# A two-block forward pass on one core: time-step products turned round, group transposes moved into the next group, gated opening loads, a tail split by token half, and six products of a tile of ones ahead of the first unit

## What is computed

```python
h = rms_norm(x, norm_w)
proj = h @ w_in
sc_b, sc_c, sc_v, sc_z, ssd_z, ssd_xbc, ssd_dt, mq, mz = _split(proj, EVEN_SPLITS)
y_a = sc_b * causal_depthwise_conv(sc_c * sc_v, sc_conv_w) * silu(sc_z)
xbc = silu(causal_depthwise_conv(ssd_xbc, ssd_conv_w) + ssd_conv_b)
dt = softplus(ssd_dt + ssd_dt_bias)                  # 32 time steps for each token
y_b = ssd_chunked(xs, dt, a, bm, cm) + xs * ssd_d    # 4 groups of 8 heads, 2 chunks of 128 tokens
y_b = group_rms_norm(y_b * silu(ssd_z)) * ssd_norm_w
y_m = memory_attention(mq, mem_n, w_mk, w_mv) * silu(mz)
return x + concatenate([y_a, y_b, y_m]) @ w_out
```

## Time and profile before

| | us |
|---|---|
| median of 3 runs (lowest, highest) | 2774.18 (2772.35, 2777.26) |
| the profiled execution's own time | 2776.7 |
| its span | 2775.2 |
| TensorE busy | 2712.0 |
| VectorE busy | 1529.3 |
| ScalarE busy | 1348.5 |

### The profile page before, as it was taken

How to read it: one execution, slowest core, us unless ns; L and a number is a source line. 1 busy time by engine, 2 the same in 40 slices (tenths; PEclk the granted TensorE clock), 3 DMA queues, 4 the chain that set the end, 5 groups by cost and what they waited for, 6 DMA issues and landing times. The chain is left out here.

```text
span 2775.2 us, 36799 instructions
## 1 busy us (share of the span) xinstructions
PE 2712.0 (98%) x12515; PEld 2256.4 (81%) x12515; DVE 1529.3 (55%) x1865; ACT 1348.5 (49%) x1775; POOL 199.4 (7%) x285
## 2 busy tenths in 40 slices
PE   8999999999999999999999999999998999999997
PEld 6788888888888888888888878888777889788886
DVE  5444455656555555554444644436776755556754
ACT  6444455654444444444444544434554445555543
POOL 2100011100000000000000001001100000121100
PEclk9999999999999999999999999999999999999998
DMA  8766666676655565556666766647656666675564
GB/s 310 268 217 217 214 228 210 197 235 216 224 197 189 182 196 187 188 192 207 218 197 216 237 207 206 218 160 242 202 193 203 233 214 213 224 268 191 175 214 157
DMA packets 161355, 586.94 MB, mean 211 GB/s; under 512 B 18928, under 2 KB 18976, under 8 KB 160496
## 3 DMA queue, kind: packets, MB, share of 16 engines
q1 hardware_dynamic: 133488, 485.55, 53.3%
q0 software_dynamic: 27776, 100.15, 10.9%
HBM read 543.63 MB, written 43.56 MB: 212 GB/s over the span
## 5 line engine op out<-in xcount | busy, mean ns | idle before, releaser
L1617 DVE TENSOR_TENSOR w_lo<-raw,w_hi 128x1024 fp32r<-128x1024 f32 x922 | 1124.0, 1224 | 979.9 <-ACT w_hi L1158 973.1
L1158 ACT ACTIVATE w_hi<-raw 128x1024 fp32r<-128x1024 f32 x922 | 968.5, 1059 | 929.6 <-PE acc L703 884.7
L701 PE MATMUL acc<-w_hi,x_t_hi 128*128 128x512 f32 (+1 forms) x2400 | 955.7, 398 | 1.0 <-DVE w_lo L1617 0.9
L703 PE MATMUL acc<-w_hi,x_t_lo 128*128 128x512 f32 (+1 forms) x2400 | 935.8, 390 | 0.0
L702 PE MATMUL acc<-w_lo,x_t_hi 128*128 128x512 f32 (+1 forms) x2400 | 934.6, 389 | 0.0
L703 PEld LDWEIGHTS acc<-w_hi,x_t_lo 128*128 128x128 f32 x2400 | 451.9, 188 | 93.8
L701 PEld LDWEIGHTS acc<-w_hi,x_t_hi 128*128 128x128 f32 x2400 | 452.7, 189 | 92.6 <-DVE w_lo L1617 3.2
L702 PEld LDWEIGHTS acc<-w_lo,x_t_hi 128*128 128x128 f32 x2400 | 452.9, 189 | 90.4 <-issue 1.9
L701 PE MATMUL acc<-w_hi,ff_t_hi 128*128 128x512 f32 x352 | 137.3, 390 | 0.0
L703 PE MATMUL acc<-w_hi,ff_t_lo 128*128 128x512 f32 x352 | 137.0, 389 | 0.0
L702 PE MATMUL acc<-w_lo,ff_t_hi 128*128 128x512 f32 x352 | 136.9, 389 | 0.0
(11 more groups left out here) (371 smaller groups left out, 2627.8 us busy)
## 6 DMA issues: line engine op xcount, KB each, us to landing
raw<-stream SPq DMA_DIRECT2D x922, 512.0 KB, 4.2
d_in<-tile POOLq DMA_DIRECT2D x20, 512.0 KB, 3.6
d_ev<-tile POOLq DMA_DIRECT2D x20, 512.0 KB, 3.7
d_x<-tile POOLq DMA_DIRECT2D x16, 512.0 KB, 4.0
...
```

The lines of the kernel that those rows point to most:

```text
L701: nc.tensor.matmul(out, a_hi, w_hi[:, s, w], start=first and c == 0, stop=False)
L703: mm = nc.tensor.matmul(out, a_lo, w_hi[:, s, w], start=False, stop=last and c == UCH - 1)
L1158: nc.scalar.activation(w_hi[:, u.slot, :], raw[:, u.slot, :], ACT.Copy).then_inc(hi_ready, 1)
L1617: nc.vector.tensor_tensor(w_lo[:, s, :], raw[:, s, :], w_hi[:, s, :].bitcast(F32), ALU.subtract).then_inc(lo_ready, 1)
```

## The change

- Opening: the loads of the memory's rows wait until 3 and 4 units are used. `norm(0)` stands ahead of the `x_c` loads in GpSimd's queue, and `x_c[n]` waits until 12 + n units are used, besides the one before it. ScalarE's and VectorE's work on them (`square`, `mem_out(0)`, `x_high`, `x_low`) moves to later units. ScalarE copies one element of `ones` first of all. TensorE makes six products of the tile `ones` (128 x 128 by 128 x 256, float32) ahead of the first unit; their result is not used.
- `dt`: the weights become the stationary operand (128 columns, of which 32 count) and 256 tokens are streamed, 48 products; VectorE copies the 32 x 256 result and TensorE transposes it twice at p = 1. The later steps move one or two units back, so `d_ac` is stored after p = 7 in place of p = 5.
- Groups: the loops over four groups are written out. The finished group is transposed at p = 2 and p = 4 of the next group (or of `eout`), four transposes each, into `ps_y`.
- The first load of `sc_in` is issued when group 3's products are made (`s_y` = 4), ahead of the last stores of `sc`.
- Tail: the last four units are done first for tokens 0 to 127, then for 128 to 255 (`last_units`), and each half is finished by itself. The weighting by `fin` is done beforehand for blocks 0 to 2; the scaling is shared by VectorE (blocks 0 and 1) and ScalarE (2 and 3); eight stores of 256 KB go out from SyncE's queue. The three units of zeros are gone.

```diff
-N_UNITS = _u + LEAD
+N_UNITS = _u
+SPLIT_T = 4
+AHEAD = 6
...
+        out_v = halves(io["out"])
+        for t in range(TH):
+            for b in (0, 2, 1, 3):
+                s_ = fin_ready if b < 2 else fin_act
+                sp.wait_ge(s_, 2 * t + b % 2 + 1)
+                sp.dma_start(out_v[:, t, b * NBW:(b + 1) * NBW], res[:, b, t, :]).then_inc(fin_out, 16)
+        sp.wait_ge(fin_out, 16 * 8)
...
         pool.dma_start(tile[1][0:8, 0, 0:N_REL], io["rel_bias"]).then_inc(tile_moved[1], 16)
-        pool.wait_ge(raw_landed[0], 16)
         for b in range(2):
-            load_tile(mem_v, At(b), b % 2, [])
+            load_tile(mem_v, At(b), b % 2, [(unit_used, RING + 3 + b)])
         pool.dma_start(col2[:, :], io["conv_cols"]).then_inc(small_in, 16)
         pool.dma_start(rowb[:, :], io["rowb"].partition_broadcast(P)).then_inc(small_in, 16)
...
+        norm(0)
         for n in range(4):
+            pool.wait_ge(unit_used, RING + 12 + n)
             if n:
                 pool.wait_ge(x_in, 16 * n)
             if n == 3:
                 pool.wait_ge(turn_lo, 2 * TURN["mem"] + 2 + 2)
             pool.dma_start(x_c[n][:, :, :], io["x_cols"][:, 4 * n:4 * n + 4, :]).then_inc(x_in, 16)
-        norm(0)
         for b in range(2):
             load_tile(x_v, At(b), b, [(squared, b + 3)])
         pool.dma_start(pl_row[:, :, :], halves(io["p"])).then_inc(late_in, 16)
...
+        def load_short(j):
+            for t in range(TH):
+                pool.dma_start(sc_in[:, t, :, :].rearrange("p a n -> p (a n)"),
+                               ev_v[:, t, 6144 + 2048 * j:6144 + 2048 * (j + 1)]).then_inc(c_in, 16)
+
...
+            if last:
+                pool.wait_ge(s_y, 4)
+                all_stored(STORED["sc"] + 2)
+                load_short(0)
...
-        for j in range(2):
-            if j:
-                pool.wait_ge(c_ut, 2 * j)
-                pool.wait_ge(c_wt, 2 * j)
-            else:
-                pool.wait_ge(turn_lo, 2 * TURN["x4"] + 2)
-            for t in range(TH):
-                pool.dma_start(sc_in[:, t, :, :].rearrange("p a n -> p (a n)"),
-                               ev_v[:, t, 6144 + 2048 * j:6144 + 2048 * (j + 1)]).then_inc(c_in, 16)
+        pool.wait_ge(c_ut, 2)
+        pool.wait_ge(c_wt, 2)
+        load_short(1)
...
-        norm(7)
-        out_v = halves(io["out"])
-        for b in range(4):
-            pool.wait_ge(fin_ready, b + 1)
-            pool.dma_start(out_v[:, :, b * NBW:(b + 1) * NBW], res[:, b, :, :]).then_inc(fin_out, 16)
-        pool.wait_ge(fin_out, 64)
+        for t in range(TH):
+            pool.wait_ge(mean_ready, 8 + t)
+            pool.tensor_tensor(rstd[:, 14 + t:15 + t], mean[:, 14 + t:15 + t], expo[:, 0:1], ALU.pow)\
+                .then_inc(rstd_ready, 1)
...
+        def last_units(u, src, chunk, bank):
+
+            for n in range(SPLIT_T):
+                pe.wait_ge(lo_ready, u + n + 1 + RING)
+            for t in range(TH):
+                out = acc[2 * bank + t][:, :]
+                for n in range(SPLIT_T):
+                    for c in range(UCH):
+                        w = slice(c * NBW, (c + 1) * NBW)
+                        s = (u + n) % RING
+                        k = (chunk + UCH * n) % 20 + c
+                        a_hi = src[0][:, k, t * P:(t + 1) * P]
+                        a_lo = src[1][:, k, t * P:(t + 1) * P]
+                        nc.tensor.matmul(out, a_hi, w_hi[:, s, w], start=False, stop=False)
+                        nc.tensor.matmul(out, a_hi, w_lo[:, s, w], start=False, stop=False)
+                        mm = nc.tensor.matmul(out, a_lo, w_hi[:, s, w], start=False,
+                                              stop=n == SPLIT_T - 1 and c == UCH - 1)
+                mm.then_inc(unit_used, SPLIT_T // TH)
...
+        pe.wait_ge(ones_ready, 1)
+        for _ in range(AHEAD):
+            nc.tensor.matmul(ps_s[:, 0:TOK], ones[:, 0:P], ones[:, :], start=True, stop=True)
...
-        for t in range(TH):
-            for c in range(16):
-                w = slice(32 * c, 32 * c + 32)
-                a_hi, a_lo = (x3_t[x][:, c, t * P:(t + 1) * P] for x in range(2))
-                out = ps_y[:, 32 * t:32 * t + 32]
-                nc.tensor.matmul(out, a_hi, w_hi[:, u.slot, w], start=c == 0, stop=False)
-                nc.tensor.matmul(out, a_hi, w_lo[:, u.slot, w], start=False, stop=False)
-                mm = nc.tensor.matmul(out, a_lo, w_hi[:, u.slot, w], start=False, stop=c == 15)
+        for c in range(16):
+            w = slice(32 * c, 32 * c + P)
+            x_hi, x_lo = (x3_t[x][:, c, :] for x in range(2))
+            out = ps_y[:, 0:TOK]
+            nc.tensor.matmul(out, w_hi[:, u.slot, w], x_hi, start=c == 0, stop=False)
+            nc.tensor.matmul(out, w_lo[:, u.slot, w], x_hi, start=False, stop=False)
+            mm = nc.tensor.matmul(out, w_hi[:, u.slot, w], x_lo, start=False, stop=c == 15)
         mm.then_inc(unit_used, 1)
 
         def time_steps(p):
-            if p == 3:
-
-                pe.wait_ge(dt_v, 3)
+            if p == 1:
+                pe.wait_ge(dt_v, 1)
+                for t in range(TH):
+                    mm = nc.tensor.transpose(ps_y[:, TOK + 32 * t:TOK + 32 * t + 32], dt_t[:, t * P:(t + 1) * P],
+                                             ident[0:32, 0:32])
+                mm.then_inc(pe_once, 1)
+            if p == 5:
...
-            if p == 5:
-                pe.wait_ge(dt_v, 4)
+            if p == 7:
+                pe.wait_ge(dt_v, 5)
                 nc.tensor.transpose(ps_s[0:64, 0:P], acum[:, :], ident[:, :]).then_inc(pe_once, 1)
...
-                pe.wait_ge(dt_v, 6)
-                pe.wait_ge(turn_lo, At(TURN["sy"], i, 1).times(2, 2))
+                pe.wait_ge(dt_v, 7)
+                pe.wait_ge(s_yb, n.times(1, 1))
...
+                pe.wait_ge(turn_lo, 2 * (TURN["sy"] + g) + 2)
                 nc.tensor.matmul(ps_y[:, :], cv[:, 5, P:TOK], st[:, :], start=True, stop=True).then_inc(s_y, 1)
-            if p == 15:
-                turn_tile(At(TURN["sy"], i, 1), yb, s_tile, n.times(1, 1))
-
-        with pe.Fori(0, 4) as i:
-            pair_of("sc", 0, i, 1, 8, x3_t, 0, lambda p: ssd(p, i))
+
+        def turn_group(p, n):
+
+            for h in range(2):
+                if p == 2 + 2 * h:
+                    pe.wait_ge(s_tile, n + 1)
+                    pe.wait_ge(turn_lo, 2 * (TURN["sy"] + n) + h + 2)
+                    for c in range(2):
+                        for t in range(TH):
+                            at = (2 * h + c) * P
+                            mm = nc.tensor.transpose(ps_y[:, (c * TH + t) * P:(c * TH + t + 1) * P],
+                                                     yb[:, t, at:at + P], ident[:, :])
+                    mm.then_inc(turned, 1)
+
+        def sc_beside(p, g):
+            ssd(p, g)
+            if g:
+                turn_group(p, g - 1)
+
+        for g in range(4):
+            pair_of("sc", 2 * g, 0, 0, 8, x3_t, 0, lambda p: sc_beside(p, g))
...
+            turn_group(q, 3)
...
-            for k in range(10):
...
+        last_units(U0["oout"] + 40 - SPLIT_T, o_t, 16 + UCH * (10 - SPLIT_T), (B0["oout"] + 3) % 2)
...
-            if (b, k) in ((0, 3), (0, 4), (1, 0), (1, 1)):
-                n = ((0, 3), (0, 4), (1, 0), (1, 1)).index((b, k))
+            if (b, k) in ((0, 6), (0, 7), (1, 2), (1, 3)):
+                n = ((0, 6), (0, 7), (1, 2), (1, 3)).index((b, k))
                 act.wait_ge(xin_landed[n % 2], 16 * (n // 2 + 1))
                 square(xin[n % 2], 0, At(n), n or None)
-            if (b, k) == (1, 4):
+            if (b, k) == (1, 6):
                 mem_out(0)
-            if b in (1, 2) and k % 2 == 1:
-                x_high(4 * (b - 1) + k // 2)
-            if (b, k) in ((2, 2), (2, 4), (3, 2), (3, 4)):
-                n = ((2, 2), (2, 4), (3, 2), (3, 4)).index((b, k))
+            if b == 2:
+                x_high(k)
+            if (b, k) in ((2, 6), (2, 7), (3, 3), (3, 4)):
+                n = ((2, 6), (2, 7), (3, 3), (3, 4)).index((b, k))
                 act.wait_ge(xin_landed[n % 2], 16 * (LOADED["x"] + n // 2 + 1))
                 square(xin[n % 2], 8, At(n), 4 + n)
 
+        act.wait_ge(ones_ready, 1)
+        nc.scalar.activation(junk[:, 0:1], ones[:, 0:1], ACT.Copy).then_inc(act_once, 1)
...
-        def sc_pair(i, last_group):
+        def high_group(p, n):
+
+            for h in range(2):
+                if p == 2 + 2 * h:
+                    act.wait_ge(turned, 2 * (TURN["sy"] + n) + h + 1)
+                    for c in range(2):
+                        ch = 4 * n + 2 * h + c
+                        last = nc.scalar.activation(z_t[0][:, ch, :], ps_y[:, c * TOK:(c + 1) * TOK], ACT.Copy,
+                                                    scale=gain[:, 96 + ch:97 + ch])
+                    last.then_inc(turn_hi, 1)
...
             if p == 0:
                 summed(At(U0["dt"]))
```

(65 more changed lines are left out.)

153 lines of the change are left out of this document (89 added, 64 removed).

## The result

The changed kernel takes 2758.86 us (median of 5, 2757.64 to 2759.76) beside 2774.18 for the kernel before on the same chip: a ratio of 0.9947, 95% interval 0.9934 to 0.9959. It is faster, by 15.3 us (0.5%) where 31.1 were forecast, and the time lies above the range of 2733 to 2753. Its profiled execution has a span of 2757.1 at a granted clock of 0.993, where before had 2775.2 at 0.989.

What follows compares the result with a forecast made beforehand. TensorE was taken as the bound, 919 units making 2500 us. Terms 11.3 (dt) + 11.7 (groups) + 9.7 (short convolution) + 2.0 (tail) - 3.6 (opening) = 31.1 off 2774.2 gave 2743.1 us, range 2733 to 2753.

Steps and rivals of the forecast that it cites:

- Groups: Turns between groups: moving the transposes to p = 2 and 4 removes TensorE's waits, winning 11.7 us (6 to 13.8).
- Rival B: VectorE becomes the bound in three groups (2.5 each) and at the short convolution (wait of 4): 2751.7 us, chance 0.12.
- Opening: Start until the 28th unit: GpSimd's chain releases TensorE at 93.9 in place of 90.3, losing 3.6 us.
- the silent stream: Opening: SyncE's loads fall silent near 80 us, so the bias loads run almost alone and win 4.6 us.
- rival A: Opening: the chain in GpSimd's queue stays as long as now, losing the whole 10.8: 2750.3 us, chance 0.2.
- Six products: Ahead of the first unit: cost 0, make it 2.9 us sooner, not counted; without them, up to 2.9 later.
- dt: The dt products: 48 of 256 columns take 5.45 us in place of 96 taking 15.48, saving 11.3 (6.1 to 11.5).
- rival D: Weight loads don't overlap with products in dt, which then takes 10.7: 2748.3 us, chance 0.04.
- Short convolution: Start of the short convolution: the earlier `sc_in` load leaves a wait of 1.4 us, winning 9.7 (7 to 11).
- Tail: Kernel's end: finishing by halves saves 5.1 us, less a stand of 2.5 and 0.6 slow clock: wins 2.0 (0 to 5).
- 5.4 to the end of the span: Tail: the time from the last store's landing to the end of the span, in the kernel before.
- the two rows of memory rows: Stretches where memory rows are loaded, at `ein` and at `uq`: forecast 0 each.

Runs made afterwards that it cites:

- experiment 3: The changed kernel with the second half of each group's transposes, copies and low parts at unit 6 of the next group in place of 4: 2748.61 us, ratio 0.9906.
- experiment 6: The changed kernel with the two halves of a group's transposes at units 4 and 6 of the next group: 2761.28 us, ratio 0.9952.
- experiment 11: The changed kernel with the halves of a group's transposes at units 4 and 8 (last group's at 2 and 6): 2749.16 us, ratio 0.9911.
- experiment 4: The changed kernel without the six products of ones ahead of the first unit: 2763.21 us, ratio 0.9962.
- experiment 7: The changed kernel with its eight last stores and the wait for them in GpSimd's queue in place of SyncE's: 2763.14 us, ratio 0.9965.
- experiment 12: The kernel before with its four last stores and the wait for them in SyncE's queue in place of GpSimd's: 2768.78 us, ratio 0.9980.

## Why the prediction was wrong, point by point

- **Groups: the step that failed.** "They now stand at p = 2 and p = 4, when `yb` has long been scaled" asked only whether the source is ready. It did not ask when the target is free. The turn went from two banks to the one bank `ps_y`, so the second half waits for VectorE's low part of the first, which stands behind three rounds of taps and splits. The price was put at 0.5 a group; it was 3.4 of waiting and about 1.6 of slow transposes and products after it. With two units between the halves the wait is there, with four it is gone (experiments 3, 6 and 11). The direct test, a second bank for the second half, was not run. Rival B had VectorE as the bound, but as a late split worth 2.5, not as a bank; the bank was in no rival.
- **Opening: the path was right, a term of it was not.** The chain in GpSimd's queue did set the 28th unit, and the silent stream did win 4.7 at the bias loads where 4.6 was said. That agreement is in part luck: the 4.6 was worked out for 2 MB, and the two loads move 1.5. What failed is "the `x_c` loads, no longer beside a burst of other loads, and the power taken out of the queue I put at 2.6 together". In place of winning 2.6 this part of the chain lost 1.0: 0.8 won by the power, 1.1 at `d_skew`, and 2.8 lost at `d_e`, because the early power also took away the pause of the stream that had covered `d_e` before. The `x_c` loads, 6.7, 6.8 and 5.3 apart where 5.9 was said, and a start 0.9 later put `x_c[3]` 2.0 behind the forecast. So the release was 5.4 late, and the slow products after the longer stand cost 1.0 more than before. The number is nearly rival A's (-10.8 said, -10.1 measured), its mechanism is not: the chain was 3.7 shorter than before, and started later.
- **Six products: counted as nothing by themselves.** In the profile of the changed kernel they made the first unit fast, as said, but the other traces show that they do so only sometimes (experiment 4). The forecast's own "up to 2.9 later" without them is not contradicted; a fast first unit was worth some 2 us at the 28th.
- **dt was right** (11.3 said, 11.1 in the profile). 48 products took 5.70 where 5.45 was taken, 0.119 each, with their 48 weight loads busy for 5.67 of it, so the loads overlapped and rival D (10.7) falls. The Trainium skill's "TensorE: Matmul & The Clock Gate", section "The mechanism", has them overlap only where the row groups differ; here every product takes all rows, and the trace does not agree with that sentence. The same section allows the overlap for the background weight buffer too; which of the two it is here, the trace doesn't show.
- **Short convolution was right** (9.7 said, 9.0 in the profile). Its wait was 1.1 where 1.4 was said, and the later `sc_in` chain on VectorE was what came next.
- **Tail: right in its parts, one part unseen.** The stand of 2.5 was there (2.56), with eight slow products among those after it, 1.7 in place of 0.6. Saved on the way from TensorE's end to the last issue: 4.9, where 5.1 was said. But "5.4 to the end of the span", taken as fixed, went as well, because the last wait left GpSimd's queue: 4.6 us. Experiments 7 and 12 show it from both sides, 4.3 and 4.5 by the medians. Why the program ends later behind a wait in GpSimd's queue, no run shows.
- In the sum by the profiles: groups 12.5 short, opening 6.5 short, dt and short convolution 0.9 short, tail 3.5 over, and the two rows of memory rows 3.5 over: 12.9 of 31.1. The medians miss 15.8; the rest is the difference between profiled execution and median.
